# One run of 36 gate matmuls per chunk instead of two of 18 in the SSD stage

## The reference, cut to what matters

```python
def ssd_chunked(xh, dt, a, bmat, cmat):
    x = (xh * dt[..., None])                       # chunks of 128 tokens, 4 groups of 8 heads
    a_cs = jnp.cumsum(da, axis=2)
    decay = jnp.exp(jnp.where(tri, seg, -jnp.inf))
    cb = jnp.einsum("bclgn,bcsgn->bcgls", cm, bm)
    w_intra = cb[:, :, :, None] * decay
    y_diag = jnp.einsum("bcgrls,bcsgrp->bclgrp", w_intra, x)
    states = jnp.einsum("bcsgn,bcgrs,bcsgrp->bcgrpn", bm, decay_to_end, x)
    _, prev = lax.scan(step, h0, (states, chunk_decay))   # h * dec + st, chunk after chunk
    y_off = jnp.einsum("bclgn,bcgrpn,bcgrl->bclgrp", cm, prev, jnp.exp(a_cs))
    return y_diag + y_off

proj = u @ w_in[layer]                             # its last 3072 columns are the gate logits
gates = jax.nn.sigmoid(gate_logits)
merged = gates[0] * (y_sb @ w_sb_out) + gates[1] * (y_ssd @ w_ssd_out) + gates[2] * (y_mem @ w_mem_out)
```

## Time and profile before

| | us |
|---|---|
| median of three runs | 2852.52 |
| the runs | 2849.68 to 2852.73 |
| span of the profiled execution | 2851.7 |
| PE busy in it | 2723.9 (96%) |
| DVE busy | 1502.1 (53%) |
| ACT busy | 972.0 (34%) |
| POOL busy | 1438.5 (50%) |
| the SSD stage, from PE's first to DVE's last operation | 1168.7 to 1580.8 |

### The profile page before, as it was taken

How to read it: one execution, slowest core, us unless ns; L and a number is a source line. 1 busy time by engine, 2 the same in 40 slices (tenths; PEclk the granted TensorE clock), 3 DMA queues, 4 the chain that set the end, 5 groups by cost and what they waited for, 6 DMA issues and landing times. The chain is left out here.

```text
span 2851.7 us, 34579 instructions
## 1 busy us (share of the span) xinstructions
PE 2723.9 (96%) x13268; PEld 2268.3 (80%) x13268; DVE 1502.1 (53%) x1523; ACT 972.0 (34%) x1679; POOL 1438.5 (50%) x777
## 2 busy tenths in 40 slices
PE   6999979999999999799999699999899999999998
PEld 5888868888888888588888577788687888888886
DVE  5100036776677666588888566633265334334343
ACT  4100134444444444576766345432241101101002
POOL 2466435445444544388878534456116535435443
PEclk9999989999999999899999899999999999999999
DMA  3444244243424341567666534333222111111113
GB/s 126 153 166 150 104 114 124 89 137 93 126 89 126 104 126 45 150 197 208 191 203 183 211 140 155 141 135 124 104 111 89 52 38 60 45 45 59 37 48 115
DMA packets 169122, 335.96 MB, mean 118 GB/s; under 512 B 15489, under 2 KB 96001, under 8 KB 168961
## 3 DMA queue, kind: packets, MB, share of 16 engines
q1 hardware_dynamic: 168960, 333.76, 36.2%
HBM read 244.97 MB, written 88.74 MB: 117 GB/s over the span
## 5 line engine op out<-in xcount | busy, mean ns | idle before, releaser
L948 POOL TENSOR_TENSOR sb_beta<-sb_beta,sb_rest 128x128 f32<-128x128 f32 (+7 forms) x128 | 164.1, 1282 | 380.6 <-DVE sb_rest L1004 380.6
L786 PE MATMUL sb_psg<-uh,sb_wh 128*128 128x512 f32 x768 | 306.9, 400 | 12.9 <-POOL sb_wl L934 12.9
L786 PE MATMUL sb_psg<-uh,sb_wl 128*128 128x512 f32 x768 | 313.1, 408 | 0.0
L786 PE MATMUL sb_psg<-ul,sb_wh 128*128 128x512 f32 x768 | 306.7, 399 | 0.0
L2189 POOL TENSOR_TENSOR ff_mh<-ff_w,one 128x1024 fp32r<-128x1024 f32 x32 | 73.4, 2295 | 399.1 <-PE ff_ps L2242 305.2
L1004 DVE TENSOR_TENSOR_SCAN sb_rest<-sb_rest 128x128 f32<-128x128 f32 (+7 forms) x128 | 181.7, 1419 | 138.4 <-ACT sb_rest L896 137.6
L1738 PE MATMUL mg_ps<-mg_yh,mg_wh 128*128 128x512 f32 x512 | 207.7, 406 | 28.0 <-DVE mg_yl L1943 27.3
L2360 ACT ACTIVATE ff_sq<-ff_ps 128x1024 f32<-128x1024 f32 x32 | 32.9, 1028 | 519.2 <-PE ff_ps L2242 519.2
L2466 DVE TENSOR_TENSOR ff_total<-ff_ps,ff_total 128x1024 f32<-128x1024 f32 x112 | 137.0, 1223 | 133.1 <-PE ff_ps L2278 132.3
L1738 PE MATMUL mg_ps<-mg_yh,mg_wl 128*128 128x512 f32 x512 | 202.4, 395 | 0.0
L1738 PE MATMUL mg_ps<-mg_yl,mg_wh 128*128 128x512 f32 x512 | 202.0, 395 | 0.0
(11 more groups left out here) (279 smaller groups left out, 7211.5 us busy)
## 6 DMA issues: line engine op xcount, KB each, us to landing
sb_w<-in_w_in SPq DMA_DIRECT2D x48, 512.0 KB, 5.1
scratch_proj<-sb_out SPq DMA_DIRECT2D x48, 512.0 KB, 3.0
sb_k<-scratch_qk SPq DMA_DIRECT2D x64, 256.0 KB, 6.3
ssd_arow<-scratch_decay SPq DMA_DIRECT2D x32, 512.0 KB, 5.4
mg_w<-in_w_branch SPq DMA_DIRECT2D x32, 512.0 KB, 4.3
mg_raw<-scratch_y SPq DMA_DIRECT2D x32, 512.0 KB, 5.0
mg_gate<-scratch_proj SPq DMA_DIRECT2D x32, 512.0 KB, 3.3
ff_w<-in_w_up SPq DMA_DIRECT2D x32, 512.0 KB, 3.4
```

The lines of the kernel that those rows point to most:

```text
L786: last = nc.tensor.matmul(ps_g[:, h], l[:, s, k], r[:, k, h * HALF:(h + 1) * HALF], start=(k == 0 and j == 0), stop=(k == KB - 1 and j == 2))
L948: nc.gpsimd.tensor_tensor(beta[:, i % 3, 0:cols], beta[:, i % 3, 0:cols], rest[:, i % 3, 0:cols], ALU.mult).then_inc(weighted, 1)
```

## The change

PE's list alone is changed. A chunk's two `project` calls, which stood on both sides of the back of the chunk before, now follow each other behind front(n) and back(n-1). In chunk 0, which has no back before it, nothing moves.

```diff
             for n in range(N):
                 front(n)
-                project(2 * n)
                 if n:
                     back(n - 1)
+                project(2 * n)
                 project(2 * n + 1)
             back(N - 1)
```

## The result

The changed kernel takes 2861.2 us (median of 20 runs, 2855.1 to 2870.3) where the kernel before takes 2853.3 (20 runs beside it). The ratio is 1.0024, 95% interval 1.0018 to 1.0030: slower by 0.24%, 6.9 us. One of the 20 runs before, of 3082.3 us, fell into a slower state of the chip and is not in the ratio. The forecast was 2859.0 in a range of 2854.0 to 2865.0, slower.

A forecast was written before the change was run, and what follows sets the result against it. The prediction took a DVE, ACT and POOL loop as the bound, with PE running ahead. Boundaries 3.8 plus end 2.8 made 6.6 us; 6.5 added to the 2852.5 median gave 2859.0 us, range 2854.0 to 2865.0.

The forecast's parts named there:

- PE runs ahead of a loop and isn't the bound: SSD stage: DVE, ACT and POOL form a loop that runs as long as PE, busy 99.9 of 101 us.
- The room for `stl`: Time from front's start to `psoff` on PE falls from 6.5 to 2.2 us; 27 chunks used 2.25 to 7.44.
- Removed wait: PE's 3.4 us of waits on ACT's evacuation of gate halves should go; counted 0, as PE isn't the bound.
- Chunk 2: PE idles 5.3 us at `psoff(1)` instead of 0.84, waiting for the late `stl(0)`.
- The slow spell: After chunk 2's wait PE's clock falls to its lower level: +1.5 us, 0 to 3.1.
- The boundaries: DVE set back at chunks 9, 17 and 25: 6.15 us, 7.6 with the spell; half taken, +3.8 us.
- The waits between the boundaries: `psoff` waits 0.1 to 2.1 us for `stl` in 15 chunks, costing PE only lead.
- ACT's later evacuations: In odd chunks ACT's evacuation moves from F + 3.6 to F + 7.0, hidden by its waits for `state`: 0.
- The end: Last chunk: 36 gates instead of 18 lie between T'(30) and F'(31): +2.8 us, at least +1.5.
- (a): Absorbed: late DVE finds POOL and ACT done, little beyond the end arrives: +1.5 to +5.7, 2856.0 us; chance 0.33.
- (b): PE was the bound after all: 3.4 us of evacuation waits go, nothing replaces them: 2849.1 us; chance 0.09.
- (c): Clock falls often: three more spells of 1.5 us at chunks 13, 21, 29: +10.4 to +15, 2864.5 us; chance 0.10.

The follow-up runs named there:

- the light kernels: Kernel before and changed kernel, each with 144 of 1152 gate matmuls left out: before 2856.1 us against 2855.4 full, stage 413.2; changed, stage 412.5 us.
- the first pair: First traces of the unchanged kernel before and the changed kernel, stages 412.0 and 418.3 us; the second pair repeats both, 409.9 and 418.5 us.

## Why the prediction was right, point by point

- *PE runs ahead of a loop and isn't the bound*: right. Taking 33.6 us off PE took nothing off the kernel. It holds for this kernel as it stands, and by little: with gate weight 2 loaded earlier, PE becomes the bound, 6 us lower.
- *The same work on PE, 0 within 0.1 us a chunk*: right. A chunk in which PE doesn't wait takes 12.73 us in the old order and 12.71 in the joined one.
- *The clock at its upper level in the stage*: read too generously. The two slices of the strip at the stage's ends show an 8, and the granted clock from 1168 to 1187 us is 0.82; from 1187 us on it is 1.00. No term hangs on it.
- *The room for `stl` falls from 6.5 to 2.2 us and every chunk used more*: right for the trace it was read from, where the least was 2.25 us; in the second trace of the kernel before, chunks 18, 19 and 27 use 1.6, 0.8 and 2.15. With 36 gates behind the back, `cb` starts 0.6 to 3.3 us after F in all chunks from 3 on in both traces, where it was 0.6 to 5.7 (after chunk 2). What is left of the lead is at most 3.3 us, and in 13 chunks of the first trace under 0.8.
- *Removed wait 3.4 us, counted 0*: it went. That it brought nothing by itself no run isolates; the light kernels, in which 33.6 us less of PE's work brought nothing, speak for it.
- *Chunk 2*: expected 5.3 us of idling, measured 4.85 and 4.70.
- *The slow spell*: expected 1.5 us, measured more: from the stall's end to F(3) it took 1212.17 - 1199.52 = 12.65 us where 2.03 + 8.4 = 10.4 were reckoned at the upper clock, so 2.2 us, within its 0 to 3.1. DVE stood still for 1.95 us for it at chunk 3, where the prediction had DVE not minding yet.
- *The boundaries*: the set-back at `cb(31)`, expected 3.8 us (0 to 7.6), is 3.5 in the first pair and 5.8 in the second. That half of 7.6 lies between them is luck as much as reckoning. At chunk 9 it is 5.2 and 4.7 us: 2.55 was reckoned without the spell, whose 2.2 come on top. Where DVE wins back was only guessed. It does so right behind the boundary: from `cb(9)` to `cb(10)` it takes 11.9 and 12.0 us where it took 13.5 and 14.8, and after chunk 25 (79.6 and 77.8 us from there to `cb(31)` before, 77.1 and 77.0 after).
- *The waits between the boundaries*: this step failed, and with it the sign that `stl` would be waited for in ten or more chunks. I had some 12 us in 15 chunks after chunk 2, from DVE's traced intervals; 4.0 in 6 and 4.4 in 7 came. I had halved the set-backs but left DVE's traced intervals whole when I reckoned the waits; with the interval behind chunk 9 shorter by 1.6 to 2.8 us, `stl` comes earlier for the whole group. That they cost PE only lead was wrong too: few as they are, these waits keep the joined order from winning back what chunk 2 loses (table above).
- *ACT's later evacuations at 0*: right: 37.6 us of new waiting there, DVE's wait for `sth` unchanged.
- *The end*: expected +2.8 us, measured +2.8 in both pairs. The working as written, 10.4 - 7.3 - 0.4, gives 2.7, and the sum then 6.5, which is what was added to the median.
- *Sum*: 6.6 us against 7.5 in the stage. Not in the sum were the 2.6 us by which the rest of the kernel is shorter in both traces; why, stays open. Measured by the ratio the whole is 6.9 us. So the mechanism holds; that the total comes within 0.4 us of the 6.5 added is partly luck, with one term halved by guess and some 12 us of waits where 4 came.
- *Rivals*: (a), absorbed, was the nearest; DVE did win back 0.8 to 2.5 us in the last group, but 3.5 us or more and the end's 2.8 stayed. (b) fell with the light kernels. (c) didn't come: one spell in chunk 2, none at chunks 13, 21 and 29, whose waits were 0 to 1.0 us. The Trainium skill, "Perfetto Trace Analysis", section "Identifying the Most-Contended Engine", says to optimize the engine with the highest occupancy first; read by PE's busy share, that rule points at PE here, and the trace doesn't bear it out: 33.6 us off PE left the stage at 413.2 us.

## What to carry to other kernels

An engine that is busy 99% of a stage can still be ahead of the others. Read for each hand-over how early the result was there: the smallest of these margins is what a reordering may spend, and here an edit that removed PE's only repeated wait spent 4.3 us where `stl` had come 1.0 to 5.7 us early (chunk 3 on, both traces before). Before an engine's independent work is put together in one run, look for the wait that the split run was covering; 12 of 36 matmuls in front of it were enough here.

## What the runs showed of the hardware that I had not expected

The same wait of PE, 1.7 us at the same matmul of a later stage, was followed by a spell at the lower clock in six of the fourteen traces, both of the kernel before among them, and by none in the other eight. A wait of 1.11 us in chunk 2 (the kernel joined from chunk 3 on) was followed by one, a wait of 2.33 us there (the light kernel before) was not. A wait's length alone doesn't tell whether the clock falls. And one DMA issued 7 us earlier at the start of a stage of 410 us took some 6 us off it in the trace, though its late arrival holds up ACT only once: the loop of the kernel before doesn't make that time good.
